# Eight section pieces loaded in a row at the program's head; parameter rows and router weights behind the second feature's weights

## The chip, the cores and the metric

One core of one Trainium2 chip runs the kernel. The metric is the device time of one execution in microseconds; the median of three runs stands for a kernel. Times inside the text are counted from the start of the profiled span.

## What is computed

The reference is two layers of a decoder trunk on 512 tokens of width 1024, in float32. What the change touches is the start of each layer:

```
mod = silu(c) @ ada_w[l] + ada_b[l]            # 1024 x 6144, six sections of 1024
sh1, sc1, gt1, sh2, sc2, gt2 = split(mod, 6)
h = rmsnorm(x, norm_mix[l]) * (1 + sc1) + sh1
proj = h @ w_in[l]                             # hq, hf, hi, hg, mla, diff, swa, gates
y = gated sum of four mixers(proj); x += gt1 * (y @ w_out[l])
h2 = rmsnorm(x, norm_ffn[l]) * (1 + sc2) + sh2
x += gt2 * moe(h2)                             # router_w, router_bias shared by the layers
```

The small parameters (norm gains, query and key gains, sinks, lambda) are a few hundred numbers per layer.

## The kernel before, in words

The kernel is written engine by engine, each with its own instruction list, and all waits are semaphores set by hand. The work is unrolled over the two layers. Activations lie in SBUF as eight chunks of 128 features by 512 tokens (X, H). Weights of w_in come through a ring of four places of 1 MB (256 columns each, four DMAs of 256 KB, `load`, L595); ACT copies each place to its rounded high part (`split_high`, L1488), DVE takes the low part (`split_low`, L1955), and a product is three matmuls. The first feature products are hf 0, hf 1, hq 0 and hq 1, which fill the four places; the load of hi 0 waits until hf 0's place is free.

**The head of the program.** Two sections of `mod` are needed for `h`: shift (section 0) and scale (section 1). In layer 0 both come as four pieces of 1 MB: the scale pieces into TM and DQK (`row_load`, L630), the shift pieces into Y (`rows_of_ada(0, 0, ...)`).

- PE takes the scale pieces by `mod_part` (a stationary column of silu(c), 512 moving columns, eight matmuls a piece): pieces 0 and 1, then the mean of squares (`diag`, which waits for DVE), then pieces 2 and 3. ACT copies the resulting row (L1571).
- DVE first waits for the positions and both halves of lbz (`seteven_loaded`, L1982), makes the angles for the rotary tables, takes Y piece 0 (`ada_early`), the `diag` tiles (L2050), Y pieces 1 to 3 and the table lbt.
- ACT issues the loads of c, positions and lbz on its own DMA queue (L1507 to L1512). They go element by element, 4 bytes each: 1024, 512 and twice 512 of them.

Each layer then starts with this on PE (L1238 on): wait for the parameters (`params_loaded`), transpose of pcols (ada_b and the two norm gains, 64 rows), in layer 1 the squares and three warming products, `row_section(0)` and `section(1, 1)` (one-column matmuls that turn the two sections to columns), five warming products, and the features. `warm(n, b)` issues n products of 128x256 that nobody reads; a float32 product counts as two instructions, so five are ten rows of the trace. `row_section` waits until DVE has copied the transposed pcols to colT (L2265). DVE's `feature_norm` makes H, ACT's `shift` its high part, DVE's `h_low` (L2083) the low part, chunk by chunk; the first product waits for chunk 0.

**SP's list** (L577 on) orders all loads of the queue q1: four of x, then for each i the scale piece i and the shift piece i. Behind the first pair stands `params(0)`: nine parameter rows, each spread over 128 partitions (L640), three loads of pcols (L643), and then router weights and bias (L651, L653). Behind the fourth pair come the ring's loads. In layer 1 `params(1)` is issued during the experts of layer 0.

`param_count` (L266) is the count of `params_loaded` that PE and DVE wait for at the start of each layer. DVE reads the parameter rows for the first time behind its hg copies (L2334).

Of the kernel before, what the change touches and what calls it, by code (L numbers as in the profile page):

```python
# [13 lines left out]
P = 128  # L14
D, S, DEPTH = 1024, 512, 2
NT, NC = S // P, D // P
# [248 lines left out]

def param_count(l):  # L266

    return 48 + 16 * len(ROWS) + (32 if l == 0 else 0)


def loads(slot):
# [9 lines left out]
def build(nc, a, out, rate):  # L281

    with ExitStack() as ctx:
# [28 lines left out]
        bias_row = sb("bias_row", NE)  # L312
# [53 lines left out]
        def signal(name):  # L366
            return ctx.enter_context(nc.semaphore(name))
# [25 lines left out]

        y_loaded, lifted = signals("y_loaded", NT), signals("lifted")

        c_loaded = signal("c_loaded")
        ident_ready = signal("ident_ready")

        (inputs_loaded, seteven_loaded, params_loaded, out_stored) = (signal(n) for n in (
# [175 lines left out]
        def _(eng):  # L575
# [53 lines left out]

                rows_of_ada(l, 1, i, late_ada[i], row_loaded[i])  # L630

            def params(l):

                eng.wait_ge(params_used, p.so_far(params_used))
                p.mark(params_used)
                for name, w in ROWS:
                    src = a[name][bass.ds(l, 1)]
                    if len(src.shape) == 3:
                        src = src.rearrange("a b c -> a (b c)")
                    eng.dma_start(row(name), src.partition_broadcast(P).rearrange("p a w -> p (a w)")).then_inc(  # L640
                        params_loaded, p.gives(params_loaded, 16))
                for lo, name, n in ((0, "ada_b", 48), (48, "norm_mix", NC), (56, "norm_ffn", NC)):
                    eng.dma_start(pcols[lo:lo + n, :],  # L643
                                         a[name][bass.ds(l, 1)].rearrange("a (k p) -> (a k) p", p=P)).then_inc(
                        params_loaded, p.gives(params_loaded, 16))
            for i in range(NT):
                row_load(0, i)
                rows_of_ada(0, 0, i, flat(Y[:, i]), early_loaded[i])
                if i == 0:
                    params(0)  # L650
                    eng.dma_start(rw[:, :, :], a["router_w"].rearrange("(k p) e -> p k e", p=P)).then_inc(  # L651
                        params_loaded, p.gives(params_loaded, 16))
                    eng.dma_start(bias_row[:, :], a["router_bias"].rearrange("(a e) -> a e", a=1)  # L653
                                  .partition_broadcast(P).rearrange("p a e -> p (a e)")).then_inc(
                        params_loaded, p.gives(params_loaded, 16))
            for l in range(DEPTH):

                w_in = layer("w_in", l)
# [23 lines left out]
                for key in RING_ORDER:  # L682
                    kind, i = key
                    if key == ("c", 2):
                        eng.wait_ge(stage_done, p.next(stage_done))
                        alone()
                        uq, ukv = layer("mla_w_uq", l), layer("mla_w_ukv", l)
                        for k in range(2):
                            eng.dma_start(w_uq[:, k], uq[k * P:(k + 1) * P, :]).then_inc(even_loaded, p.gives(even_loaded, 16))
                            eng.dma_start(w_ukv[k], ukv[:, k * 512:(k + 1) * 512]).then_inc(  # L690
                                even_loaded, p.gives(even_loaded, 16))
                    if kind == "ada":
                        if i >= RING:
                            ada_load(l, key)
                    elif kind == "branch":
                        if i >= 4:
                            eng.wait_ge(gates_used, p.next(gates_used))
                            alone()
                            gate_load(i - 2)
                        if i == 4:  # L700
                            eng.wait_ge(x_spilled, p.next(x_spilled, 16))
                            alone()
                            eng.dma_start(flat(X[:, :, :]), x_dram).then_inc(x_back, p.gives(x_back, 16))
                        load(key, branch(i), l)
                        if i == 3:
                            for n in range(2):
                                eng.wait_ge(gates_stored[n], p.given(gates_stored[n]))
                                alone()
                            eng.wait_ge(stage_done, p.next(stage_done))
                            alone()  # L710
                            gate_load(0)
                            gate_load(1)
                            late(0)
                            eng.wait_ge(stage_done, p.next(stage_done))
                            alone()
                            late(1)
                        if i in (5, 6):
                            late(i - 3)
                    elif key == ("out", 0):
                        for q in (6, 7):  # L720
                            eng.wait_ge(gates_used, p.next(gates_used))
                            alone()
                            gate_load(q)
                        load(key, cols(layer("w_out", l), 0, 256), l)
                    elif kind == "out":
                        load(key, cols(layer("w_out", l), i * 256, 256), l)
                    else:
                        if kind == "gate":
                            j, n = ring_place(l, key)
                            due[n * RING + j] = (2 * i, 2 * i + 1)  # L730
                        load(key, cols(w_in, COL[FIRST[kind]] + i * 256, KVR + ROPE if kind == "ckv" else 256), l)
                p.mark(gates_used, 2)
                def expert(b, m):

# [26 lines left out]
                if l + 1 < DEPTH:  # L761
                    done_at = p.so_far(expert_used) - len(RELEASES) + 1
                    for i in range(RING - 1):
                        eng.wait_ge(expert_used, done_at + last_use({j: at for at, j in slot_ring.items()}[
                            ring_place(l + 1, ("ada", i))[0]]))
                        alone()
                        ada_load(l + 1, ("ada", i))
                    params(l + 1)
                    for i in range(RING):
                        eng.wait_ge(expert_used, done_at + last_use(ROW_PLACES[i]))  # L770
                        alone()
                        row_load(l + 1, i)
                    i = RING - 1
                    eng.wait_ge(expert_used, done_at + last_use({j: at for at, j in slot_ring.items()}[
                        ring_place(l + 1, ("ada", i))[0]]))
                    alone()
                    ada_load(l + 1, ("ada", i))
# [9 lines left out]
        def _(eng):  # L787
# [36 lines left out]
            def warm(n, b):  # L824

                free(b)
                for _ in range(n):
                    mm(bank(b, 2 * P), ident[:, :], flat(lmask[:, 0:2]))
# [407 lines left out]
            for l in range(DEPTH):  # L1236

                free(0)  # L1238
                eng.wait_ge(params_loaded, p.next(params_loaded, param_count(l)))
                alone()  # L1240
                turn(ps[:, 0, 0:NCOLP], pcols[0:NCOLP, :], k=NCOLP, last=True).then_inc(
                    filled[0], p.gives(filled[0]))
# [1 line left out]
                if l:  # L1244
                    for c in range(NC):
                        square_sum(c)
                    warm(3, 5)
                row_section(0)
                section(1, 1)
                warm(5, 5)  # L1250
# [57 lines left out]

                warm(5, 5)
                free(6)  # L1310
                for k in range(NC):
                    eng.wait_ge(h_ready, p.next(h_ready))
                    ins = mm(ps[0:NE, 6], rw[:, k], H[:, k], k == 0, k == NC - 1, last=k == NC - 1)
# [581 lines left out]
        def _(eng):  # L1895
# [76 lines left out]
            def alone():  # L1972

                eng.sem_inc(waited, 1)
# [287 lines left out]
            for l in range(DEPTH):  # L2262
# [2 lines left out]
                v.tensor_copy(colT[:, :], bank(0, NCOLP)).then_inc(emptied[0], p.gives(emptied[0]))  # L2265
                eng.wait_ge(emptied[0], p.given(emptied[0]))

                eng.wait_ge(params_loaded, p.next(params_loaded, param_count(l)))
                v.tensor_copy(lic[:, :], pick(litab[:, :, :], l)).then_inc(vector_step, p.gives(vector_step))
                eng.wait_ge(vector_step, p.given(vector_step))  # L2270
                v.tensor_copy(lbc[:, :], pick(lbt[:, :, :], l)).then_inc(vector_step, p.gives(vector_step))
# [59 lines left out]
                for u in range(2):  # L2331
                    even_tiles(lambda t: TM[:, t, u * 256:(u + 1) * 256])
                    split_low(("hg", u))
                for name, n, s in (("mla_qk_norm", QKD, QKD ** -0.5), ("diff_qk_norm", HD, HD ** -0.5),  # L2334
                                   ("swa_qk_norm", HD, HD ** -0.5)):
                    v.tensor_scalar(row(name, 0, n), row(name, 0, n), s, None, ALU.mult).then_inc(
                        vector_step, p.gives(vector_step))
                    eng.wait_ge(vector_step, p.given(vector_step))
# [568 lines left out]
```

## Time and profile before

| what | value |
|---|---|
| median of three runs | 2412.09 us (2410.64 to 2412.85) |
| the profiled execution | 2409.06 us |
| its span | 2407.3 us |
| mean granted clock of TensorE | 0.972 of full |
| PE busy | 2268.8 us, 94% |
| DVE, ACT, POOL busy | 1411.2, 1005.3, 342.0 us |
| first product of layer 0, of layer 1 | 55.78, 1240.04 us |

The timeline of an engine lists its instructions, merged where alike: start, length, line, output and inputs; behind "idle before" stands what ended the wait. PEclk is the share of full clock that was granted: 1.00 is 2.4 GHz and 0.50 is 1.2 GHz. DMA issues are lines of SPq and ACTq; their length is the time in which the queue's issuer is held, not the transfer. The packets of a queue are those that its transfers were cut into.

### The profile page before, as it was taken

What the parts mean: (1) busy time and instruction counts of PE and PEld (TensorE: products, weight loads), DVE (VectorE), ACT (ScalarE), POOL (GpSimd) and SP (SyncE); (2) the same over time, 40 slices, a digit from 0 to 9 for tenths busy, and PEclk for the clock granted to TensorE, in tenths of its full rate; (3) what the DMA queues carried; (4) which work ended last, traced back from release to release, by engine and by line L of the source; (5) the groups of instructions that cost most, each with busy time, mean ns of one, the idle gap of its engine ahead of it and who ended that gap; (6) DMA issues with size and microseconds to landing.
All of it is one profiled execution on the core that took longest, in us unless ns stands there. A gap on an engine that the chain in (4) does not pass through costs nothing. (4 is left out here: it accounts for less than half of the span.)

```text
span 2407.3 us, 32310 instructions
## 1 busy us (share of the span) xinstructions
PE 2268.8 (94%) x11840; PEld 1703.4 (71%) x11840; DVE 1411.2 (59%) x2657; ACT 1005.3 (42%) x1876; POOL 342.0 (14%) x334
## 2 busy tenths in 40 slices
PE   6999989999899999999899999989988999999997
PEld 3897887786675466777569878877866744677775
DVE  4737765736654635666656477666275455366664
ACT  4423333534453124666335333345344422346662
POOL 2002200000001210444200121000000022024440
PEclk8999999999999999999989999989999999999999
DMA  8221322232216653766643222321322184536652
GB/s 292 88 82 59 96 88 88 66 93 74 75 62 232 211 196 126 290 241 240 234 140 90 88 59 88 123 75 42 95 84 75 58 310 148 227 108 251 245 194 111
DMA packets 192314, 333.67 MB, mean 139 GB/s; under 512 B 30624, under 2 KB 149280, under 8 KB 175904
## 3 DMA queue, kind: packets, MB, share of 16 engines
q1 hardware_dynamic: 169376, 305.33, 37.2%
q0 software_dynamic: 19296, 19.98, 2.6%
q10 hardware_dynamic: 3488, 6.30, 0.7%
q8 instruction: 97, 1.59, 0.3%
q14 instruction: 57, 0.47, 0.1%
HBM read 352.48 MB, written 51.38 MB: 168 GB/s over the span
## 5 line engine op out<-in xcount | busy, mean ns | idle before, releaser
L811 PE MATMUL ps<-H_rounded,WH_rounded 128*128 128x512 f32 x768 | 308.5, 402 | 0.0
L1955 DVE TENSOR_TENSOR ring_rounded<-ring,WH_rounded 128x512 fp32r<-128x512 f32 (+2 forms) x168 | 195.2, 1171 | 186.0 <-ACT WH_rounded L1488 185.8
L811 PE MATMUL ps<-X_rounded,WH_rounded 128*128 128x512 f32 x640 | 288.0, 450 | 13.4 <-ACT CM L1540 6.4
L811 PE MATMUL ps<-WH_rounded,X_rounded 128*128 128x256 f32 (+1 forms) x960 | 281.5, 293 | 17.5 <-issue 16.5
L811 PE MATMUL ps<-ring_rounded,X_rounded 128*128 128x256 f32 (+1 forms) x960 | 278.2, 290 | 0.0
L811 PE MATMUL ps<-WH_rounded,H_rounded 128*128 128x256 f32 (+1 forms) x960 | 277.7, 289 | 0.0
L811 PE MATMUL ps<-X_rounded,ring_rounded 128*128 128x512 f32 x640 | 253.1, 395 | 0.0
L811 PE MATMUL ps<-Y,ring 128*128 128x512 f32 x512 | 221.2, 593 | 1.9 <-ACT Y L1600 1.9
L1488 ACT ACTIVATE WH_rounded<-ring 128x512 fp32r<-128x512 f32 (+2 forms) x168 | 163.6, 985 | 141.2 <-PE ps L811 67.3
L2821 POOL TENSOR_TENSOR M<-M,SC 128x512 f32<-128x512 f32 x48 | 63.2, 1318 | 1092.7 <-DVE SC L2486 1092.7
L811 PEld LDWEIGHTS ps<-WH_rounded,X_rounded 128*128 128x128 f32 x960 | 192.0, 200 | 21.2 <-issue 19.6
L811 PEld LDWEIGHTS ps<-ring_rounded,X_rounded 128*128 128x128 f32 x960 | 192.0, 200 | 0.6 <-issue 0.5
L811 PEld LDWEIGHTS ps<-WH_rounded,H_rounded 128*128 128x128 f32 x960 | 191.5, 199 | 0.0
L811 PEld LDWEIGHTS ps<-Y,ring 128*128 128x128 f32 x512 | 96.8, 190 | 121.9 <-issue 121.9
L811 PEld LDWEIGHTS ps<-X_rounded,WH_rounded 128*128 128x128 f32 x640 | 121.4, 190 | 79.4 <-issue 37.2
L811 PEld LDWEIGHTS ps<-H_rounded,WH_rounded 128*128 128x128 f32 x768 | 146.2, 190 | 32.2 <-issue 6.7
L811 PEld LDWEIGHTS ps<-X_rounded,ring_rounded 128*128 128x128 f32 x640 | 121.6, 190 | 28.3
L811 PE MATMUL ps<-Y,SC 128*128 128x64 f32 (+1 forms) x512 | 133.1, 398 | 0.4 <-ACT SC L1623 0.4
L1611 ACT ACTIVATE SC<-ps,nmax 128x256 f32<-128x256 f32 (+3 forms) x192 | 94.1, 492 | 80.3 <-DVE nmax L2147 79.5
L2805 POOL TENSOR_TENSOR Y<-M,Y 128x256 f32<-128x256 f32 x56 | 48.9, 876 | 481.4 <-ACT Y L1764 312.5
L811 PE MATMUL ps<-lmask,ident 128*128 128x256 f32 x402 | 106.8, 420 | 4.1 <-issue 3.1
L809 PEld LDWEIGHTS ps<-ident,SC 128*128 128x128 f32 (+1 forms) x452 | 63.7, 153 | 64.2 <-issue 21.0
(381 smaller groups left out, 4438.6 us busy)
## 6 DMA issues: line engine op xcount, KB each, us to landing
ring<-in_w_in SPq DMA_DIRECT2D x272, 256.0 KB, 4.0
ring<-in_ada_w SPq DMA_DIRECT2D x80, 256.0 KB, 4.9
Y<-in_moe_w_down SPq DMA_DIRECT2D x18, 1024.0 KB
ring<-in_w_branch SPq DMA_DIRECT2D x64, 256.0 KB, 5.1
ring<-in_moe_w_down SPq DMA_DIRECT2D x14, 1024.0 KB, 6.8
TM<-in_ada_w SPq DMA_DIRECT2D x12, 1024.0 KB, 11.0
DQK<-in_ada_w SPq DMA_DIRECT2D x12, 1024.0 KB, 11.5
gate_logits<-CM SPq DMA_DIRECT2D x44, 256.0 KB, 2.7
```

What stands on the lines that cost most here:

```text
L809: ins = nc.tensor.transpose(o, lhsT, rhs)
L811: ins = nc.tensor.matmul(o, lhsT, rhs, start=start, stop=stop)
L1488: act(high[i][:, at:at + size], ring[:, j, at:at + size], ACT.Copy).then_inc(high_ready[i], p.gives(high_ready[i], 4 if parts is None else 1))
L1611: act(probs[n % 2][i][:, 0:w], bank(b, w), ACT.Exp, bias=nmax[:, n % 2, i:i + 1], accum_out=total).then_inc((handed if s.kind == "diff" el ...
L1955: ins = v.tensor_tensor(low[j][:, at:at + size], ring[:, j, at:at + size], high[i][:, at:at + size].bitcast(F32), ALU.subtract)
L2805: eng.tensor_tensor(half(hgQs[i], j, 1), half(hgQ[:, pr], j, 1), half(hgE[i], j, 1), ALU.mult).then_inc(qs_ready[i], p.gives(qs_ready[i]))
L2821: eng.tensor_tensor(m, m, SC[:, j], ALU.add).then_inc(added[j % 2], p.gives(added[j % 2]))
```

## The change

- SP issues the eight section pieces one after the other. Only the three loads of pcols (`param_cols`) stand among them, behind the second pair.
- The nine parameter rows (`param_rows`), the router's weights and the router's bias are issued in layer 0 behind the load of hq 1.
- The columns have a semaphore of their own, `cols_loaded`; PE waits for it ahead of the transpose. DVE's wait for `params_loaded` moves from the start of the layer to the first use of the rows, and PE gets one ahead of the router's product.
- In layer 1 the rows are issued ahead of the columns, and no longer in one function with them; the place in SP's list is the old one.
- PE has eight more warming products ahead of `row_section(0)`, in both layers.

```diff
@@ def param_count(l)
-    return 48 + 16 * len(ROWS) + (32 if l == 0 else 0)
+    return 16 * len(ROWS) + (32 if l == 0 else 0)
@@ sync
+            def param_cols(l):
+                for lo, name, n in ((0, "ada_b", 48), (48, "norm_mix", NC), (56, "norm_ffn", NC)):
+                    eng.dma_start(pcols[lo:lo + n, :], ...).then_inc(
+                        cols_loaded, p.gives(cols_loaded, 16))
+            def param_rows(l):
                 for name, w in ROWS:
...
+            def params_free():
+                eng.wait_ge(params_used, p.so_far(params_used))
+                p.mark(params_used)
+            params_free()
             for i in range(NT):
                 row_load(0, i)
                 rows_of_ada(0, 0, i, flat(Y[:, i]), early_loaded[i])
-                if i == 0:
-                    params(0)
-                    eng.dma_start(rw[:, :, :], ...)
-                    eng.dma_start(bias_row[:, :], ...)
+                if i == 1:
+                    param_cols(0)
...
                         load(key, cols(w_in, ...), l)
+                    if l == 0 and key == ("hq", 1):
+                        param_rows(0)
+                        eng.dma_start(rw[:, :, :], ...)
+                        eng.dma_start(bias_row[:, :], ...)
...
-                    params(l + 1)
+                    params_free()
+                    param_rows(l + 1)
+                    param_cols(l + 1)
@@ tensor
                 free(0)
-                eng.wait_ge(params_loaded, p.next(params_loaded, param_count(l)))
+                eng.wait_ge(cols_loaded, p.next(cols_loaded, 48))
                 alone()
                 turn(ps[:, 0, 0:NCOLP], pcols[0:NCOLP, :], k=NCOLP, last=True)
...
                     warm(3, 5)
+                warm(8, 5)
                 row_section(0)
                 section(1, 1)
                 warm(5, 5)
...
                 free(6)
+                eng.wait_ge(params_loaded, p.next(params_loaded, param_count(l)))
+                alone()
                 for k in range(NC):
@@ vector
-                eng.wait_ge(params_loaded, p.next(params_loaded, param_count(l)))
                 v.tensor_copy(lic[:, :], pick(litab[:, :, :], l))
...
                     split_low(("hg", u))
+                eng.wait_ge(params_loaded, p.next(params_loaded, param_count(l)))
```

## Rows read from the trace of the kernel before

**Rows 1.** The page: busy us of each engine and share of the span.

```profile
PE 2268.8 (94%) x11840; PEld 1703.4 (71%) x11840; DVE 1411.2 (59%) x2657; ACT 1005.3 (42%) x1876; POOL 342.0 (14%) x334
```

**Rows 2.** Timeline of PE, 17 to 56 us.

```profile
26.11 6.24 PE L811 MATMUL ps<-TM,cact 128*1 128x512 f32 x8 [4.66 <-DMA TM<-in_ada_w]
32.28 1.16 PE L811 MATMUL ps<-SC,ones 128*128 128x128 f32 x8
33.37 7.03 PE L811 MATMUL ps<-DQK,cact 128*1 128x512 f32 x16
...
45.21 3.56 PE L811 MATMUL ps<-ones,spare 1*128 1x1 f32 x16 [4.61 <-DVE colT L2265]
48.70 3.58 PE L811 MATMUL ps<-ones,SC 128*128 128x1 f32 x16
...
55.78 0.58 PE L811 MATMUL ps<-X_rounded,WH_rounded 128*128 128x512 f32 x1
```

**Rows 3.** Timeline of DVE, 21 to 56 us.

```profile
21.33 0.16 DVE L1984 TENSOR_TENSOR lbw<-lbz 128x4 f32<-128x4 f32 x1 [21.33 <-DMA lbz<-in_hg_lb_logits]
...
28.72 0.87 DVE L2050 TENSOR_SCALAR SC<-ident,ssq 128x128 f32<-128x128 f32 x4
...
41.29 2.74 DVE L2040 SCALAR_TENSOR_TENSOR SC<-Y,cact,SC 128x512 f32<-128x512 f32 x4 [4.78 <-DMA Y<-in_ada_w]
...
54.38 0.75 DVE L2083 SCALAR_TENSOR_TENSOR H_rounded<-H,mod,X_rounded 128x512 fp32r<-128x512 f32 x1 [0.19 <-ACT X_rounded L1578]
```

**Rows 4.** Waits, 0 to 60 us: us in total, times, longest.

```profile
ACT WH_rounded L1488 <- DMA ring<-in_w_in: 6.9, 2, 5.8
```

**Rows 5.** SP's issues in the timeline; last, DVE's first use of the rows.

```profile
4.04 0.50 SPq L640 DMA_DIRECT2D rows<-in_hg_onorm  x1
...
15.96 1.50 SPq L653 DMA_DIRECT2D bias_row<-in_router_bias  x1
...
22.31 0.51 SPq L626 DMA_DIRECT2D Y<-in_ada_w  x1
...
38.83 10.61 SPq L603 DMA_DIRECT2D ring<-in_w_in  x11
...
L2336 DVE TENSOR_SCALAR rows<-rows x3: 195/196/204, 129.7 to 130.1; 128x64 f32<-128x64 f32 x2, 128x96 f32<-128x96 f32 x1
```

**Rows 6.** Window: busy us by engine, PEclk, DMA share, GB/s last.

```profile
35.00:36.00 1.00, 1.00 (x4) 0.23 (x3) 1.00 (x3) 1.00 (x1) 0.00 (x0) 1.00 1.02 410
```

**Rows 7.** Packets, MB, share by queue, in 0:24, 0:12, 8:12, 4:6.

```profile
q10 hardware_dynamic: 2624, 0.01, 6.2%
...
q10 hardware_dynamic: 1282, 0.01, 5.9%
...
q1 hardware_dynamic: 421, 1.59, 98.5%
q10 hardware_dynamic: 421, 0.00, 6.0%
...
q10 hardware_dynamic: 611, 0.00, 16.8%
```

**Rows 8.** Windows in which the granted clock fell and came back.

```profile
24.00:25.00 1.00, 0.00 (x0) 0.00 (x0) 0.87 (x4) 0.59 (x4) 0.00 (x0) 0.82 0.97 377
...
31.00:32.00 1.00, 1.00 (x3) 0.13 (x1) 1.00 (x2) 0.00 (x0) 0.00 (x0) 0.77 1.03 410
```

**Rows 9.** Start of layer 1: timelines of PE and DVE, a window.

```profile
1232.62 1.94 PE L811 MATMUL ps<-ones,spare 1*128 1x1 f32 x16
...
1236.30 4.09 PE L811 MATMUL ps<-lmask,ident 128*128 128x256 f32 x10
1240.04 0.58 PE L811 MATMUL ps<-X_rounded,WH_rounded 128*128 128x512 f32 x1
...
1234.68 2.29 DVE L1955 TENSOR_TENSOR ring_rounded<-ring,WH_rounded 128x2048 fp32r<-128x2048 f32 x1 [12.95 <-ACT WH_rounded L1488]
...
1236.00:1240.00 4.00, 4.00 (x13) 3.27 (x14) 3.68 (x8) 1.72 (x3) 0.00 (x0) 0.57 0.00 0
```

More of the change, by code:

```diff
@@ L394, in build @@
         y_loaded, lifted = signals("y_loaded", NT), signals("lifted")
-        c_loaded = signal("c_loaded")
+        c_loaded, cols_loaded = signal("c_loaded"), signal("cols_loaded")
         ident_ready = signal("ident_ready")
@@ L630, in row_load @@
                 rows_of_ada(l, 1, i, late_ada[i], row_loaded[i])
-            def params(l):
-                eng.wait_ge(params_used, p.so_far(params_used))
-                p.mark(params_used)
+            def param_cols(l):
+                for lo, name, n in ((0, "ada_b", 48), (48, "norm_mix", NC), (56, "norm_ffn", NC)):
+                    eng.dma_start(pcols[lo:lo + n, :],
+                                         a[name][bass.ds(l, 1)].rearrange("a (k p) -> (a k) p", p=P)).then_inc(
+                        cols_loaded, p.gives(cols_loaded, 16))
+            def param_rows(l):
                 for name, w in ROWS:
@@ L641, in params @@
                         params_loaded, p.gives(params_loaded, 16))
[L642 to L645, printed above, removed]
+            def params_free():
+                eng.wait_ge(params_used, p.so_far(params_used))
+                p.mark(params_used)
+            params_free()
             for i in range(NT):
@@ L648, in _ @@
                 rows_of_ada(0, 0, i, flat(Y[:, i]), early_loaded[i])
-                if i == 0:
-                    params(0)
[L651 to L655, printed above, removed]
+                if i == 1:
+                    param_cols(0)
             for l in range(DEPTH):
@@ L731, in _ @@
                         load(key, cols(w_in, COL[FIRST[kind]] + i * 256, KVR + ROPE if kind == "ckv" else 256), l)
+                    if l == 0 and key == ("hq", 1):
+                        param_rows(0)
+                        eng.dma_start(rw[:, :, :], a["router_w"].rearrange("(k p) e -> p k e", p=P)).then_inc(
+                            params_loaded, p.gives(params_loaded, 16))
+                        eng.dma_start(bias_row[:, :], a["router_bias"].rearrange("(a e) -> a e", a=1)
+                                      .partition_broadcast(P).rearrange("p a e -> p (a e)")).then_inc(
+                            params_loaded, p.gives(params_loaded, 16))
                 p.mark(gates_used, 2)
```

## The prediction

> **What bounds the kernel now.** The page comes first [rows 1]: PE is busy for 94% of the span. The change touches the start of each of the two layers, so what counts is when a layer's first product (128x512, of hf 0) can start; behind it all engines follow at their old distances, and I carry a shift there unchanged to the end. I read the head of the program in the timelines of PE and DVE, then the waits, SP's issues, the DMA rate, the packets of the two queues and the granted clock, and the start of layer 1 last.
>
> Layer 0's first product starts at 55.78 [rows 2]. Ahead of it PE has two pieces of the scale section (the second at 26.11, after 4.66 us of waiting), the mean of squares at 32.28, the other two pieces (33.37 to 40.4), the transpose of pcols, a wait of 4.6 for colT until 45.21, 16 one-column matmuls for each of the two sections, and five warming products. DVE [rows 3]: its first instruction waits for lbz until 21.33; the set-up, Y piece 0 and the diagonals end at 29.59, 8.26 later; Y pieces 1 to 3 take 2.74 each, and the last waits 4.78 for its data, until 41.29. ACT waits 5.8 us for the ring's first load [rows 4]. So **late loads bound the head**, and they are late because SP issues 14 small transfers, from 4.04 to 17.46, between the first pair of pieces and the second; the last piece goes out at 22.8 [rows 5]. Once all are queued, DMA moves 410 GB/s [rows 6].
>
> **What the loads gain.** At half a microsecond each [rows 5], eight pieces and three column loads are issued by about 9 us, or as the queue drains. At 0.40 MB/us [rows 6], 2 MB of x and eight of pieces are in after about 2.5 + 10/0.40 = 27.5 us, the first ring load by 31. Each beats its user below, so I price the waits for Y, for colT and for the ring (4.8, 4.6, 5.8) as gone, and ask what is late next. The eleven parameter and router loads stand now behind hq 1. They hold SP for 11.7 us (13.4 less 1.7 for the columns), over by 61 even if the ring's loads leave no sooner than now, at 49.4 [rows 5]. The next ring load waits for hf 0's place, free when its 48 matmuls of 0.213 us have ended, 10 us behind a first product near 54: no earlier than 64. DVE reads the rows first at 129.7 [rows 5]. Cost nothing; if that cover went, hi 0 would come late by the excess. In layer 1 the columns only change places with the rows: nothing.
>
> **What is late next: lbz.** It goes by ACT's queue (q10) in elements of 4 bytes: c, positions and lbz are 2624 packets [rows 7]. While SP's queue (q1) has 4 KB packets, the two take turns packet by packet: 421 and 421 in the four us from 8 to 12. By 12 us 1282 of ACT's have gone, and nothing differs up to there, since x and the first pair are ahead in both kernels. The other 1342 now meet 4 KB packets until the end: 1342 / (421/4) = 12.8 us, the last at 24.8, and DVE starts at 25.2. Bounds: 21.33 (no delay) and 25.2. I take the upper, the rate of the same two queues and the same packets. DVE: diagonals end at 25.2 + 8.26 = 33.5; three Y pieces 8.2, the table lbt 0.9: free at 42.6, and not just ahead of 45.2.
>
> The Trainium skill, page "DMA: Bandwidth & Descriptors", section "Queues, rings and completion order", says that an engine takes turns between queues by packets, a packet being typically 9 to 17 descriptors. By that, small descriptors would pass in groups and lbz would hardly be late; the equal counts of 8 to 12 us speak against it.
>
> **PE.** The scale section's second piece is in by about 16, so it follows the first directly: 21.45 (26.11 less the 4.66 of waiting) to 25.0. Then PE idles 8.5 us for the diagonals. The idle that began at 21.45 saw the granted clock fall at 24.6 (mean 0.82 from 24 to 25), and it came back at 31.5, 5.4 us after the second piece began [rows 8]. In layer 1 it was low from 1236.2 and back before 1240, 3.4 us after warming began [rows 9]. So the mean, 1.16 us at full clock [rows 2] and some 2.1 at half, ends at 35.6, and of the 16 matmuls of pieces 3 and 4 those before 36.9 to 38.9 take 0.85 us and the rest 0.43 (6.24 for eight at mostly half, 7.03 for sixteen at full): one to four of them at the long time. They end at 35.6 + 16 x 0.43 + 0.42 x (1 to 4) = 42.9 to 44.2; I take **43.6**. Now it is 40.4, so this is 3.2 us later. DVE's 42.6 is hidden beside it.
>
> Behind it: transpose 0.2; the eight new warming products, 16 instructions of 256 columns at 0.213 us, 3.4; the two sections. These took 3.49 and 3.58 at half clock [rows 2], but 1.9 each in layer 1 right behind a warming [rows 9]; I take layer 1's, as the new warming stands in the same place: 3.7. Then the five warming products: in layer 1 the clock had fallen by then, and they took 3.75. First product at 43.6 + 0.2 + 3.4 + 3.7 + 3.75 = **54.7**, against 55.78: **1.1 us gained**. If the clock holds, the chain through DVE and ACT from the sections' end to the first H_lo binds (52.28 to 55.13, 2.85 [rows 2, 3]): 53.8, 2.0 gained.
>
> **Layer 1** gets the same eight products at 1232.62, where PE does not wait: it goes from three warming products straight into the sections [rows 9]. Cover would be DVE's split of hf 0, over at 1236.97, 0.5 us behind PE's sections; but the five warming products end with the start of the first product at 1240.04, so PE is the bound. Cost 3.4 us, or 2.7 if the last warming then runs at full clock and the chain of H takes over. I take 3.4, the row nearest.
>
> **Sum:** -1.1 + 3.4 = +2.3 us (with the kinder clock -2.0 + 2.7 = +0.7). The profiled execution took 2409.06 us for a span of 2407.3; the median of three runs is 2412.09, 3.0 above it, and I put the difference on the median: **2414.4 us**. That is 0.1% slower, within the 0.2% (4.8 us) that a measurement of this kernel can tell.
>
> **Rivals.**
> 1. *lbz on time.* For it: from 4 to 6 us 611 of ACT's packets passed [rows 7], three times the later rate, so the turns are not one for one everywhere. Against: the equal counts of the loaded stretch. Diagonals at 29.6, mean 31.7, pieces end near 39.7, first product 50.8: -5.0 + 3.4 = -1.6, 2410.5. The Trainium skill's rule above would have it come out so.
> 2. *lbz on time and the clock held.* PE's idle would then be 4.6 us, and the one from 21.45 lost the clock after 3.2. Pieces end at 29.6 + 1.16 + 7.03 = 37.8, first product 10.2 later at 48.0: -7.8 + 2.7 = -5.1, 2407.0, the only case faster by over 0.2%.
> 3. *Slower: the clock stays low through pieces 3 and 4.* Their matmuls have one stationary column, and the one-column sections from 45.21 to 52.28 ran at half clock to the end [rows 2, 9]. Against: the second piece, with the same instruction, ended at full clock. Place: the 16 matmuls behind the 8.5 us idle; price 0.42 us each. All sixteen: pieces end at 49.2, first product 60.3: +4.5 + 3.4 = +7.9, 2420.0. It decides from nine of them at 0.85 us on (end past 46.0).
> 4. *The pieces land no sooner*, because SP's queue holds only so much (the 11 ring loads from 38.83 held SP for 10.6 us [rows 5]). Then DVE releases colT at 45.2 as now, the wait hides the new warming, and the sections run at full clock: 45.2 + 3.7 + 3.75 = 52.7, -3.1 + 3.4 = +0.3, 2412.4.
>
> **Chances:** forecast with its two clocks 0.56, rival 1 0.14, rival 2 0.09, rival 3 0.13, rival 4 0.03, the rest 0.05 for a shift that is not carried through the 2300 us behind. Range 2408.0 to 2418.5: it takes in the forecast's bounds (2412.1 to 2415.0: pieces ending at 42.9 with the kinder clock, at 44.2 with the other), rivals 1 and 4, and 3 up to twelve matmuls at 0.85 us. Faster 0.11, within 0.2% 0.72, slower 0.17.
>
> **What would show it.** Right: DVE's first instruction near 25; no wait for Y; the second piece directly behind the first and then an idle of about 8.5 us ahead of the mean, with a low clock at its end; ACT's split of hf 0 directly behind its copy of the row; first product of layer 0 at about 54.7; in layer 1 3.4 us more from the last update of X to the first product. Wrong: DVE starting near 21; a first product before 51 or after 57; layer 1's distance unchanged, which would mean that the warming is covered there and the change is worth what the head gains.

## The result and the profile after

The changed kernel takes 2414.89 us in the median of 20 runs, the kernel before 2410.52 us in 20 runs beside it; ratio 1.0023, 95% interval 1.0015 to 1.0031. One of the twenty runs before took 2827 us and is left out of the ratio. By the ratio the change costs 5.5 us (3.6 to 7.5; the medians lie 4.4 apart), where +2.3 was forecast. It is clear of zero, but the runs don't say on which side of the prediction's bound of 4.8 us it lies. The absolute time of 2414.89 us lies in the forecast range, beside 2414.4.

First PE in the head of the changed kernel, from its timeline (start, length, line; the helper's line is now L823). It answers to [rows 2].

```profile
18.45 7.03 PE L823 MATMUL ps<-TM,cact 128*1 128x512 f32 x16
36.49 2.04 PE L823 MATMUL ps<-SC,ones 128*128 128x128 f32 x8 [11.02 <-DVE SC L2065]
38.46 8.57 PE L823 MATMUL ps<-DQK,cact 128*1 128x512 f32 x16
46.97 0.27 PE L821 MATMUL ps<-ident,pcols 64*128 64x64 f32 x1
47.17 3.72 PE L823 MATMUL ps<-lmask,ident 128*128 128x256 f32 x16
50.82 1.94 PE L823 MATMUL ps<-ones,spare 1*128 1x1 f32 x16
52.69 1.95 PE L823 MATMUL ps<-ones,SC 128*128 128x1 f32 x16
54.50 3.88 PE L823 MATMUL ps<-lmask,ident 128*128 128x256 f32 x10
57.82 0.99 PE L823 MATMUL ps<-X_rounded,WH_rounded 128*128 128x512 f32 x1
```

The two first pieces run without a gap, then PE waits 11 us for DVE's diagonals. The first product comes at 57.82 and not at 55.78. The order is the forecast one, only each time from 36.49 on is some three us later. DVE's timeline (the lines that answer to [rows 3]) says why:

```profile
28.07 0.16 DVE L1999 TENSOR_TENSOR lbw<-lbz 128x4 f32<-128x4 f32 x1 [28.07 <-DMA lbz<-in_hg_lb_logits]
...
35.48 0.87 DVE L2065 TENSOR_SCALAR SC<-ident,ssq 128x128 f32<-128x128 f32 x4
36.26 8.03 DVE L2055 SCALAR_TENSOR_TENSOR SC<-Y,cact,SC 128x512 f32<-128x512 f32 x12
...
47.35 0.23 DVE L2280 COPY colT<-ps 128x64 f32<-128x64 f32 x1 [2.19 <-PE ps L821]
```

All twelve instructions of Y 1 to Y 3 stand in one row with no wait between them: the loads are on time. The wait that replaced theirs is the first one, for lbz. The packets of ACT's queue in 0:12, 12:16, 16:20, 20:24 and 24:28 (packets, MB, share), the answer to [rows 7]:

```profile
q10 hardware_dynamic: 1281, 0.01, 5.9%
...
q10 hardware_dynamic: 392, 0.00, 6.0%
...
q10 hardware_dynamic: 481, 0.00, 7.3%
...
q10 hardware_dynamic: 370, 0.00, 5.9%
...
q10 hardware_dynamic: 100, 0.00, 1.5%
```

Two windows of the same kernel, 28 to 36 and 42 to 50 us (busy us by engine, then PEclk, DMA share, GB/s), answer to [rows 8]: half clock through the idle, full clock from within pieces 3 and 4 to the sections. It fell once more in the last warming (0.63 from 55 to 56).

```profile
28.00:36.00 8.00, 0.00 (x0) 0.00 (x0) 7.20 (x30) 0.50 (x2) 0.00 (x0) 0.50 1.07 365
...
42.00:50.00 8.00, 8.00 (x26) 3.50 (x25) 4.02 (x13) 3.51 (x4) 0.00 (x0) 1.00 0.88 332
```

Layer 1, PE's timeline, beside [rows 9]:

```profile
1221.14 0.24 PE L821 MATMUL ps<-ident,pcols 64*128 64x64 f32 x1 [1.03 <-DVE X L2571]
...
1231.69 4.91 PE L823 MATMUL ps<-lmask,ident 128*128 128x256 f32 x22
1236.54 1.94 PE L823 MATMUL ps<-ones,spare 1*128 1x1 f32 x16
1238.41 2.44 PE L823 MATMUL ps<-ones,SC 128*128 128x1 f32 x16
1240.70 4.62 PE L823 MATMUL ps<-lmask,ident 128*128 128x256 f32 x10
1244.76 0.99 PE L823 MATMUL ps<-X_rounded,WH_rounded 128*128 128x512 f32 x1
```

From the transpose of pcols to the first product (the distance, below) it is 23.6 us here and was 19.3 before. The stretches between (layer 0's first product to layer 1's transpose, 1163.3 here and 1165.0 before) differ by several us from execution to execution of any of these kernels (1159.6 to 1168.4 over all the profiles). So I read the two heads from the profiles and the sum from the timed runs.

### The profile page after: what moved, and what is told of

Its sections match the earlier page's. It is cut to its first block, busy times and chain, and to the rows that moved or that the text cites. A ratio compares the mean times of both kernels' runs of the same rounds, so it can differ in the third digit from the quotient of the medians.

```text
span 2412.5 us, 32376 instructions
## 1 busy us (share of the span) xinstructions
PE 2263.8 (94%) x11872; PEld 1700.7 (70%) x11872; DVE 1411.9 (59%) x2657; ACT 1003.1 (42%) x1876; POOL 341.7 (14%) x334
## 4 chain that ended last, share of the span: by engine, by line
PE 80%; DVE 9%; ACT 4%; issue 3%; DMA 3%; SPq 0%; POOL 0%; ACTq 0%; POOLq 0%; DVEq 0%
PE ps L823 75%; PE ps L821 5%; DVE ssq L2105 1%; DMA lbz<-in_hg_lb_logits 1%; DVE ring_rounded L1970 1%; DVE nmax L2162 1%; DMA ring<-in_w_in 1%; ACT WH_rounded L1503 1%; DVE ps L2159 1%; ACT SC L1626 1%; DVE spare L1952 0%; DVE X L2571 0%; DVE DQK L2107 0%; DMA M<-h_rows,find_i 0%; ACT rsq L1598 0%
## 5 line engine op out<-in xcount | busy, mean ns | idle before, releaser
L823 PE MATMUL ps<-H_rounded,WH_rounded 128*128 128x512 f32 x768 | 309.2, 403 | 0.0
L823 PE MATMUL ps<-X_rounded,WH_rounded 128*128 128x512 f32 x640 | 289.7, 453 | 13.3 <-ACT CM L1555 6.5
L823 PE MATMUL ps<-WH_rounded,X_rounded 128*128 128x256 f32 (+1 forms) x960 | 279.1, 291 | 17.5 <-issue 16.4
L823 PE MATMUL ps<-ring_rounded,X_rounded 128*128 128x256 f32 (+1 forms) x960 | 276.4, 288 | 0.0
L823 PE MATMUL ps<-WH_rounded,H_rounded 128*128 128x256 f32 (+1 forms) x960 | 275.9, 287 | 0.0
L823 PE MATMUL ps<-X_rounded,ring_rounded 128*128 128x512 f32 x640 | 253.8, 397 | 0.0
L823 PE MATMUL ps<-Y,ring 128*128 128x512 f32 x512 | 221.2, 593 | 1.9 <-ACT Y L1615 1.9
L823 PEld LDWEIGHTS ps<-WH_rounded,X_rounded 128*128 128x128 f32 x960 | 189.6, 197 | 21.2 <-issue 19.6
L823 PEld LDWEIGHTS ps<-ring_rounded,X_rounded 128*128 128x128 f32 x960 | 189.7, 198 | 0.6 <-issue 0.5
L823 PEld LDWEIGHTS ps<-WH_rounded,H_rounded 128*128 128x128 f32 x960 | 189.4, 197 | 0.0
L823 PEld LDWEIGHTS ps<-Y,ring 128*128 128x128 f32 x512 | 97.0, 190 | 121.6 <-issue 121.6
L823 PEld LDWEIGHTS ps<-X_rounded,WH_rounded 128*128 128x128 f32 x640 | 122.7, 192 | 79.9 <-issue 37.6
L823 PEld LDWEIGHTS ps<-H_rounded,WH_rounded 128*128 128x128 f32 x768 | 147.3, 192 | 32.4 <-issue 7.0
L823 PEld LDWEIGHTS ps<-X_rounded,ring_rounded 128*128 128x128 f32 x640 | 122.2, 191 | 28.1
L823 PE MATMUL ps<-Y,SC 128*128 128x64 f32 (+1 forms) x512 | 134.1, 401 | 0.4 <-ACT SC L1638 0.4
L823 PE MATMUL ps<-lmask,ident 128*128 128x256 f32 x434 | 110.7, 409 | 4.1 <-issue 3.1
```

What stands on the lines that cost most here:

```text
L823: ins = nc.tensor.matmul(o, lhsT, rhs, start=start, stop=stop)
```

## The experiments

Ratios are to the kernel before, timed beside each version. Of each edit the main lines are shown, and a line of words stands for the code that it names. Where the text tells of a load's parts, it goes by the packed trace, which has 16 updates of the semaphore for each of these loads.

**Without the eight warming products** in both layers.

```diff
-                warm(8, 5)
                 row_section(0)
```

> The changed kernel without the eight extra warming products in both layers. Theory A (each of them stands on PE's path): layer 1's first product comes 3.4 to 4.3 us earlier after the last update of X, layer 0's about 2 to 3.4 us earlier (sections straight behind the transpose at full clock; ACT's row copy and DVE's colT then cost 0.5), 5 to 7 us off the changed kernel: at or 1 us under the kernel before. Theory B (the warming pays for itself through the clock, and the order of the loads makes the kernel slower): no gain, the sections and the first products run at half clock instead, time within 1 us of the changed kernel.

Ratio 0.9986 (0.9973 to 0.9999): 3.4 us under the kernel before, barely clear of noise, and about 9 under the changed kernel. PE's timeline:

```profile
45.27 0.27 PE L821 MATMUL ps<-ident,pcols 64*128 64x64 f32 x1
45.93 1.94 PE L823 MATMUL ps<-ones,spare 1*128 1x1 f32 x16 [0.39 <-DVE colT L2279]
47.80 2.46 PE L823 MATMUL ps<-ones,SC 128*128 128x1 f32 x16
50.12 4.62 PE L823 MATMUL ps<-lmask,ident 128*128 128x256 f32 x10
54.18 0.99 PE L823 MATMUL ps<-X_rounded,WH_rounded 128*128 128x512 f32 x1
```

The row section takes 1.94 us, as with the warming: pieces 3 and 4 had brought the clock up already. Transpose to first product is 8.9 us and not 10.9: in layer 0 the warming of 3.7 us costs 2.0, because without it PE waits 0.4 us for colT, and the clock falls sooner (at 49.1, in the second section), so that the last warming runs at half clock throughout. In layer 1 the distance is 20.2. Theory A holds: both warmings stand on the path, and the new order of the loads alone is a small gain.

**The warming in layer 0 only.**

```diff
-                warm(8, 5)
+                if l == 0:
+                    warm(8, 5)
```

> The changed kernel with the eight extra warming products in layer 0 only. Theory A: layer 0 as in the changed kernel (first product near 57.8), layer 1 as before, 3.4 to 4.3 us off the changed kernel, 1 to 2 us over the kernel before. Theory B: layer 1's first product no earlier, no gain.

Ratio 1.0012 (0.9999 to 1.0025), some 2.7 us under the changed kernel. First product at 57.84, as in the changed kernel; layer 1's distance 19.2. Over all profiles the distance is 22.7 to 23.6 in the five kernels with the warming in layer 1 (mean 22.9) and 19.2 to 20.3 in the seven without (mean 19.6): it costs 3.4 us there.

**The kernel before with the warming alone.**

```diff
                     warm(3, 5)
+                warm(8, 5)
                 row_section(0)
```

> The kernel before with the eight extra warming products and nothing else. In layer 0 PE waits 4.6 us for colT, so the warming is hidden and the two sections run at full clock (1.9 us each and not 3.5): the first product 1 to 3 us earlier, held by the split of hf 0 that ended at 51.1. Layer 1: 3.4 to 4.3 us later. Theory A: +1 to +3 us in all. Theory B: 0 or faster by up to 3.

Ratio 1.0026 (1.0009 to 1.0043), +6.3 us: more than either theory gave. PE's timeline, then the last piece of shift on DVE:

```profile
39.64 3.72 PE L811 MATMUL ps<-lmask,ident 128*128 128x256 f32 x16
48.57 3.57 PE L811 MATMUL ps<-ones,spare 1*128 1x1 f32 x16 [5.21 <-DVE colT L2266]
52.07 3.58 PE L811 MATMUL ps<-ones,SC 128*128 128x1 f32 x16
...
44.66 2.74 DVE L2041 SCALAR_TENSOR_TENSOR SC<-Y,cact,SC 128x512 f32<-128x512 f32 x4 [8.59 <-DMA Y<-in_ada_w]
```

The warming is hidden in the wait for colT, but it stands at the wait's front: 5.2 us of idle follow it, and the sections run at half clock all the same. Layer 1's distance is 22.7.

Y 3 came at 44.66 in this execution, 3.4 us later than in [rows 3]. What delayed it is ACT's store of x, 2 MB to x_cols, which ACT issues behind PE's mean. Its issue, and the queues in one of the microseconds in which it passes, first in the kernel before (39 to 40), then here (36 to 37):

```profile
34.20 0.35 ACTq L1698 DMA_DIRECT2D x_cols<-X  x1
...
q10 hardware_dynamic: 25, 0.41, 95.5%
q1 hardware_dynamic: 27, 0.03, 9.4%
...
32.32 0.35 ACTq L1699 DMA_DIRECT2D x_cols<-X  x1
...
q10 hardware_dynamic: 23, 0.38, 88.1%
q1 hardware_dynamic: 16, 0.07, 16.0%
```

The store's packets are of 16 KB and take most of the DMA time while it passes. In the kernel before, 14 of Y 3's 16 parts had landed by 37.7, and the last two came at 41.2 and 41.3. Here the store went out 1.9 us earlier and caught all 16, which landed from 40.8 to 44.6. It went out earlier for a reason that lies ahead of the warming in PE's list: the last part of c landed at 14.6 (11.6 in the kernel before), so PE began its first piece later, idled 1.25 us and not 4.66 ahead of the second, kept full clock and was at the mean 1.9 us sooner. Whether the eleven other runs went the same way is not known.

**Y 0 and the diagonals ahead of the wait for lbz**, DVE's list in the changed kernel:

```diff
-            wait for lbz and positions; rotary set-up
+            eng.wait_ge(tables_ready, p.next(tables_ready))
             ada_early(0)
             diagonals
+            wait for lbz and positions; rotary set-up
```

> The changed kernel with DVE's list turned: Y piece 0 and the diagonals ahead of the wait for lbz and the rotary set-up. If DVE's wait for lbz (28.07) is what delays the head, PE's mean starts near 25.8 right behind the second piece and not at 36.5, the clock does not fall, pieces 3 and 4 end near 34 to 35. DVE then bounds: set-up 28.1 to 33.4, Y pieces 1 to 3 to 41.6, lbt to 42.5, the section of shift behind it: first product near 50 to 52 and not 57.8, 6 to 8 us off the changed kernel. If the late lbz is not what counts, the first product stays within 1 us of 57.8.

Ratio 0.9997 (0.9983 to 1.0012). PE's timeline:

```profile
26.35 1.13 PE L823 MATMUL ps<-SC,ones 128*128 128x128 f32 x8 [0.37 <-DVE SC L2019]
27.41 7.03 PE L823 MATMUL ps<-DQK,cact 128*1 128x512 f32 x16
...
43.10 3.57 PE L823 MATMUL ps<-ones,spare 1*128 1x1 f32 x16 [4.81 <-DVE colT L2280]
```

The mean starts 10.1 us earlier, with the clock up: lbz was what held PE. But DVE now works off the set-up and Y behind lbz, colT comes at 42.8, and behind 4.8 us of idle both sections run at half clock again (3.57 us): first product 54.08, 3.7 us gained and not 6 to 8.

**c in rows**: partition p takes c[8p] to c[8p+7], and ada_w's rows are read in the same order.

```diff
-                eng.dma_start(cact[:, :], a["c"].rearrange("b (k p) -> p (b k)", p=P))
+                eng.dma_start(cact[:, :], a["c"].rearrange("b (p k) -> p (b k)", p=P))
-                w = layer("ada_w", l).rearrange("(k p) n -> p k n", p=P)
+                w = layer("ada_w", l).rearrange("(p k) n -> p k n", p=P)
...
```

> The changed kernel with c laid out so that partition p holds c[8p] to c[8p+7] (128 runs of 32 bytes in place of 1024 elements), and the rows of ada_w in the same order; same sums in another order. Theory (the queues take turns packet by packet, so lbz is late by the count of ACT's packets ahead of it): 896 fewer packets at 104 a microsecond, lbz 8.6 us earlier, DVE's first instruction near 19.5 and not 28.1, the mean near 28 to 29, pieces 3 and 4 over near 37, first product near 47.5 to 50, 7 to 9 us off the changed kernel. Rival (lbz is late because of the slow end of each small write under load, not the count): DVE starts at 26 or later.

ACT's packets in all, 0:30:

```profile
q10 hardware_dynamic: 1728, 0.01, 3.3%
```

896 fewer than [rows 7], and DVE starts at 22.60, 5.5 us earlier; the rival (26 or later) falls. It is 3 us short of the full 8.6: 842 packets had gone by 12 us, and not 1281, so of the saving only half (457 packets) was left to come. First product 51.76, 6.1 us earlier. Ratio 1.0005 (0.9992 to 1.0017), 4 us under the changed kernel.

**Pieces 3 and 4 held back until lbz is in.** One run, of which only the profile is read.

```diff
             for i in range(NT):
+                if i == 2:
+                    eng.wait_ge(seteven_loaded, 48)
+                    alone()
                 row_load(0, i)
```

> The changed kernel with SP holding pieces 3 and 4 back until lbz and the positions are in, so that ACT's small packets meet an idle queue once the 6 MB ahead are through. If turns of packets cause the delay, ACT's packets pass faster than 104 a microsecond from about 17 us on, and DVE starts near 22 to 24 and not 28; the last Y piece then lands past 33 and the head gains little. If lbz lands near 28 all the same, the turns are not the cause.

ACT's packets in 12:16, 16:20 and 19:20:

```profile
q10 hardware_dynamic: 396, 0.00, 6.1%
...
q10 hardware_dynamic: 873, 0.00, 12.8%
...
q10 hardware_dynamic: 578, 0.00, 33.0%
```

Up to 16 us the pace is that of the changed kernel (392), and up to 19 us 94 to 106 a microsecond. When the six MB ahead run out, 578 pass in one, and DVE starts at 21.64. With part of the count taken away, or the load beside it, lbz comes early: the turns are the cause. Y 3 waits only 0.84 us (its work starts at 36.0), and the first product comes at 52.70.

**Versions that beat both kernels.** No extra warming; DVE in the order Y 0, Y 1, diagonals, Y 2, lbz and set-up, Y 3:

```diff
-                warm(8, 5)
...
             ada_early(0)
+            ada_early(1)
             diagonals
+            ada_early(2)
             wait for lbz and positions; rotary set-up
-            for i in range(1, NT):
-                ada_early(i)
+            ada_early(3)
```

> The changed kernel without the extra warming, with DVE in the order Y 0, Y 1, diagonals, Y 2, wait for lbz, rotary set-up, Y 3; c as in the kernel before. lbz still near 28; set-up to 33.5, Y 3 to 36.3, colT near 37.5, first product near 44 to 47: 9 to 11 us off the kernel before. If the idle of about 3 us on PE ahead of colT costs the clock, the later figure.

First product 49.27, ratio 0.9965 (0.9952 to 0.9979). That is 2 us later than the later figure expected: PE idles 5.1 us until colT (38.0), and both sections run at half clock. With c in rows, and only Y 0 ahead of lbz:

```diff
-                warm(8, 5)
...
+            ada_early(0)
             wait for lbz and positions; rotary set-up
-            ada_early(0)
             diagonals
```

> The kernel with c in rows, without the eight extra warming products, and with DVE doing Y piece 0 ahead of its wait for lbz. If both causes hold and add: diagonals near 26, mean at full clock, pieces over near 34.5, colT near 35.5, sections 3.8, H chain 2.9: first product near 42 to 44 (55.78 before), layer 1 as before, 11 to 14 us off the kernel before, 0.5%.

First product 47.90 and not 42 to 44, ratio **0.9957** (0.9942 to 0.9972), 10 us under the kernel before. The diagonals still wait for lbz and the set-up (27.65), so PE idles 5.9 us ahead of the mean, which then runs at half clock (2.05 us).

**The warming where PE waits**: the order Y 0, Y 1, diagonals, Y 2 with the warming in layer 0 alone, here against the version above with that order.

```diff
+                if l == 0:
+                    warm(8, 5)
                 row_section(0)
```

> The kernel with Y 0 to Y 2 ahead of the wait for lbz, and eight warming products ahead of the row section in layer 0 alone. Theory (warming costs nothing where PE waits longer than it takes): PE waits 5.1 us for colT there, the warming takes 3.4, so it is hidden, the two sections run at full clock (1.9 each and not 3.6), first product near 46 to 47 and not 49.3, layer 1 as before: 2 to 3 us off that kernel. Rival: the clock falls all the same, or the warming ends behind colT: first product at 49 or later.

Ratio 0.9971 (0.9959 to 0.9983), no different from the kernel without the warming. PE's timeline, then ACT's:

```profile
33.12 3.72 PE L823 MATMUL ps<-lmask,ident 128*128 128x256 f32 x16
38.38 1.94 PE L823 MATMUL ps<-ones,spare 1*128 1x1 f32 x16 [1.54 <-DVE colT L2282]
40.25 2.61 PE L823 MATMUL ps<-ones,SC 128*128 128x1 f32 x16
...
48.25 0.76 PE L823 MATMUL ps<-X_rounded,WH_rounded 128*128 128x512 f32 x1 [0.92 <-DVE H_rounded L2100]
```

```profile
43.38 1.91 ACT L1504 ACTIVATE WH_rounded<-ring 128x2048 fp32r<-128x2048 f32 x1 [5.64 <-issue]
45.31 1.28 ACT L1560 ACT_TABLE_LOAD   x1
46.60 1.33 ACT L1594 ACTIVATE X_rounded<-H,mod 128x512 fp32r<-128x512 f32 x2
```

Hidden, and the sections end 2.5 us earlier than without it (42.9 against 45.4). But the first product gains 1.0 only: it now waits for ACT, whose split of hf 1 comes at 43.4, 5.6 us behind its last work, and ACT's high part of H stands behind that split. The view names no releaser for it ("issue"), but the last part of hf 1's load landed at 43.31. The load is late because the 2 MB of x that ACT sends out at 30.7 go beside it: from 35 to 39 us ACT's queue has 65 to 118% of the DMA time, and SP's 5 to 8%.

**All of it**: c in rows, Y 0, Y 1, diagonals, set-up, Y 2, Y 3, the warming in layer 0. DVE's list against the same version:

```diff
             ada_early(1)
             diagonals
-            ada_early(2)
             wait for lbz and positions; rotary set-up
-            ada_early(3)
+            for i in (2, 3):
+                ada_early(i)
```

> c in rows, DVE in the order Y 0, Y 1, diagonals, wait for lbz, set-up, Y 2, Y 3, eight warming products in layer 0 alone. lbz near 22.4, hidden behind the diagonals at 24.7; set-up to 30, Y 3 to 35.4, colT near 36.3; pieces 3 and 4 over at 32.9 at full clock, the warming covered. First product near 43.5 to 44.5, 11 to 12 us ahead of the kernel before, 0.5% in all.

Ratio **0.9959** (0.9945 to 0.9973), first product 47.56 and not 44. ACT's timeline:

```profile
26.43 0.35 ACTq L1714 DMA_DIRECT2D x_cols<-X  x1
...
39.67 1.91 ACT L1504 ACTIVATE WH_rounded<-ring 128x2048 fp32r<-128x2048 f32 x1 [6.42 <-DMA ring<-in_w_in]
42.69 1.91 ACT L1504 ACTIVATE WH_rounded<-ring 128x2048 fp32r<-128x2048 f32 x1 [1.10 <-DMA ring<-in_w_in]
```

The earlier the mean, the earlier x is sent out (26.4), so that its packets (29 to 35 us) go beside the last parts of Y 3 and the ring's first load: DVE waits 1.9 us for the one, ACT 6.4 for the other. A version that sends x later was not tried.

## Why the prediction was right, and where its size was off

- **The loads gain**: right that the waits go, in part for another reason. No wait for Y, and ACT's split of hf 0 came directly behind its copy of the row (47.57). The parameter loads behind hq 1 were issued from 37.1 to 49.6, and DVE did not wait for the rows at 132.1. But the prediction put the late loads down to SP's 14 small transfers alone. Of the 4.78 us that DVE waited for Y 3 in the kernel before, some 2.4 came with the store of x. That is an estimate: the last two of the 16 parts were 1.2 us behind the others in the pieces ahead of it, and 3.6 in Y 3. The ring's first load, for which ACT waited 5.8, landed in parts from 37.6 to 46.7, with the same store between them. In the changed kernel the pieces and the first two ring loads were in by 37.4, before the store passed (43 to 49 us).
- **lbz is late next**: right in kind, and the term that was mis-sized. The turns are of single packets: in the packed trace 416 of the 421 4-byte packets from 8 to 12 us of the kernel before, and 364 of 392 from 12 to 16 in the changed one, start just 5 or 6 ns ahead of a packet of SP's queue. The equal counts alone would also come out of turns of equal groups. I had 25.2 as the upper bound; it was 28.07. The pace was right as long as it was an average: 1243 packets from 12 to 24 us, 103.6 a microsecond against 105. The last hundred were not: 50 from 24 to 25, 37 in the next. The wait ends with the last of the parts, and these come apart: of the 48 updates that DVE waited for (16 for each of three loads) 40 were in by 24.9, 47 by 26.8, and the last came at 28.05. A mean rate ends before that. Before the change the last packets had passed by 21, with DVE 0.3 behind. The bound from above was no bound.
- **PE behind it**: idle 11.0 and not 8.5 us, pieces over at 47.0 and not 43.6. Of these 3.4 us, 2.9 are lbz's; the rest is that the clock came back at the late end of what was allowed for. From there the working holds: 10.8 us to the first product, 11.05 forecast, the sections at 1.9 each, the last warming mostly at half clock. Head: +2.0 instead of -1.1, so the head was forecast to gain and lost. The first product at 57.82 lies past 57, which the prediction had named as a sign of being wrong.
- **Layer 1**: 3.4 forecast, 3.4 measured as the mean over the kernels with and without it (4.3 in the one pair of profiles). PE was the bound there.
- **The sum**: 2.0 + 3.4 = 5.4, and the timed runs give 5.5. The change was forecast at less than half of that, short by the 3 us of lbz. That the absolute time came so near (2414.4, 2414.89) is luck: the kernel before has its median 1.6 us lower in 20 runs than in the three that the forecast started from.
- **Rivals**: lbz came later, not on time, so 1 and 2 fell; the equal counts that spoke against them were the right row. Rival 3 fell: the clock came back within pieces 3 and 4 (8.57 us for sixteen, so some four at 0.85). Rival 4 fell too: SP was held (2.4 to 2.7 us for each of its last three pieces), and still the pieces landed in time.

## What to carry to other kernels

A transfer in thousands of 4-byte runs has no size but a count: here each run waited for one packet of the other queue (391 beside 392 from 12 to 16 us), so filling that queue with large packets delayed it. Before packing the loads of a head, look for the small load that a first instruction waits for, cut its runs (c in rows: 1024 to 128), or put work ahead of its wait. Warming was hidden only inside a wait, and it served only near the wait's end: the first section ran at full clock with 1.5 us of idle behind the warming, and at half clock with 4.8 or 5.2. In front of sections that followed busy matmuls it cost 2.0 us in layer 0 and 3.4 in layer 1, and in an unrolled loop it is paid in every turn, also where nothing waits. A large store is a load's rival too: see where it goes out, and what it passes.

## What was not expected

- The mean rate of a queue did not give its end: half the pace and less in the last stretch, and 2.9 us later than the rate says.
- Sixteen one-column matmuls right behind pieces 3 and 4 took 1.94 us with and without the extra warming. The clock rose during pieces 3 and 4, which have one stationary column (0.50 at their start at 38.5, 1.00 from 42). It fell again in the kernel without the warming at 49.1 us, during the second section, and in the changed kernel at 55.3, during the last warming.
- What brings the mean forward brings the store of 2 MB of x forward too, into the ring's loads or, in the last version, already into Y 3. The three best heads start their first product at 47.6 to 48.3, some 8 us ahead of the kernel before. In all three ACT waits for a ring load that landed behind the store (hf 1's split at 42.7 to 43.4). That sending x later would give more is not shown.
